# Branch B's product of a hybrid encoder step: out of the eight heads, into eight units of seven block products behind the merge gates

## The reference

```python
xr, gr, xm, zm, pi, pf, ga, gb = split(u @ w_in)       # 1024,1024,2048,2048,8,8,1024,1024
y_a = rglru(conv4(xr)) * gelu(gr)                       # 1024 wide
h_m = mlstm(q, k from silu(conv4(xm)), v from xm, pi, pf)   # 8 heads x 256
y_b = sigmoid(zm) * h_m                                 # 2048 wide
mix = sigmoid(ga) * (y_a @ w_branch_a) + sigmoid(gb) * (y_b @ w_branch_b)
x = x + mix @ w_out
x = x + relu(RMSNorm(x) @ w_mlp_up)**2 @ w_mlp_down     # then a final RMSNorm
```

## Time and profile before

| | us |
|---|---|
| median of 3 runs | 2144.64 (2144.36 to 2147.55) |
| the profiled execution, first to last instruction | 2142.7 |
| TensorE busy (share) | 2128.2 (99%) |
| VectorE busy | 1441.4 (67%) |
| POOL busy | 1093.8 (51%) |
| ScalarE busy | 715.3 (33%) |
| one head, from chunk stage to chunk stage | 100.94 |
| of it, the chain's stretch of 468 matmuls | 78.18 |

### The profile page before, as it was taken

The page is one execution under the profiler, slowest core; times in us unless marked ns, Lnnn a source line. Parts: engine busy times, 40 slices in busy tenths (PEclk is TensorE's granted clock), DMA queues, the critical chain, the costliest instruction groups (busy, mean ns, idle before and its releaser), DMA issues.

```text
span 2142.7 us, 37489 instructions
## 1 busy us (share of the span) xinstructions
PE 2128.2 (99%) x14272; PEld 2106.8 (98%) x14272; DVE 1441.4 (67%) x1522; ACT 715.3 (33%) x952; POOL 1093.8 (51%) x765
## 2 busy tenths in 40 slices
PE   9999999999999999999999999999999999999998
PEld 8999999999999999999999999999999999999988
DVE  7676776147767676867676756577876646458886
ACT  5443434213232322323232311234444434424342
POOL 3556564342434343433334244448787767778740
PEclk9999999999999999999999999999999999999999
DMA  3212112431212121111212123464445446526522
GB/s 134 71 55 69 61 55 98 148 102 56 68 45 67 45 78 58 54 58 50 62 50 62 45 96 97 149 227 174 173 166 182 152 167 250 198 100 244 184 70 84
DMA packets 95953, 230.50 MB, mean 108 GB/s; under 512 B 10464, under 2 KB 16736, under 8 KB 91392
## 3 DMA queue, kind: packets, MB, share of 16 engines
q1 hardware_dynamic: 58960, 109.03, 16.3%
q10 hardware_dynamic: 36912, 120.34, 15.3%
HBM read 168.52 MB, written 60.82 MB: 107 GB/s over the span
## 4 chain that ended last, share of the span: by engine, by line
PE 94%; DVE 3%; DMA 1%; POOL 1%; issue 1%; ACT 1%; DVEq 0%; SPq 0%; POOLq 0%; ACTq 0%
PE ps L916 56%; PE ps L1199 24%; PE ps L1296 4%; PE ps L1108 2%; PE ps L1142 1%; PE ps L1123 1%; PE ps L1145 1%; DMA last_x<-hid 1%; PE ps L1150 1%; PE ps L1094 1%; DVE form_lo L2050 0%; DVE vt L2047 0%; PE ps L1095 0%; DVE acc L2050 0%; POOL wsum L802 0%
## 5 line engine op out<-in xcount | busy, mean ns | idle before, releaser
L774 POOL TENSOR_TENSOR w_hi<-w_raw,ones 128x512 fp32r<-128x512 f32 x216 | 261.0, 1208 | 807.3 <-PE ps L916 761.4
L777 POOL TENSOR_TENSOR w_lo<-w_raw,w_hi 128x512 fp32r<-128x512 f32 x216 | 336.7, 1559 | 16.9
L916 PE MATMUL ps<-u_hi,w_hi 128*128 128x364 f32 x1521 | 337.8, 330 | 1.5 <-issue 0.6
L916 PE MATMUL ps<-u_hi,w_lo 128*128 128x364 f32 x1521 | 335.7, 329 | 0.0
L916 PE MATMUL ps<-u_lo,w_hi 128*128 128x364 f32 x1521 | 335.2, 328 | 0.0
L916 PEld LDWEIGHTS ps<-u_hi,w_hi 128*128 128x128 f32 x1521 | 263.8, 188 | 3.0 <-issue 1.2
L916 PEld LDWEIGHTS ps<-u_lo,w_hi 128*128 128x128 f32 x1521 | 264.5, 188 | 0.0
L916 PEld LDWEIGHTS ps<-u_hi,w_lo 128*128 128x128 f32 x1521 | 264.4, 188 | 0.0
L1199 PE MATMUL ps<-form_hi,hi 128*128 128x272 f32 x784 | 162.1, 288 | 0.4 <-POOL lo L799 0.4
L1199 PE MATMUL ps<-form_hi,lo 128*128 128x272 f32 x784 | 162.3, 288 | 0.0
L1199 PE MATMUL ps<-form_hi,w_hi 128*128 128x272 f32 x776 | 161.4, 289 | 0.8 <-DVE small L2050 0.4
(11 more groups left out here) (354 smaller groups left out, 4509.7 us busy)
## 6 DMA issues: line engine op xcount, KB each, us to landing
w_raw<-in_w SPq DMA_DIRECT2D x280, 256.0 KB, 2.6
form_lo<-hid_forms ACTq DMA_DIRECT2D x21, 1088.0 KB, 7.8
rstd<-in_w SPq DMA_DIRECT2D x50, 256.0 KB, 2.7
hid_forms<-acc ACTq DMA_DIRECT2D x12, 816.0 KB, 6.0
bc<-out_rows ACTq DMA_DIRECT2D x8, 1092.0 KB, 6.1
hid_forms<-stage ACTq DMA_DIRECT2D x6, 1088.0 KB, 4.4
hid_forms<-acc ACTq DMA_DIRECT2D x12, 544.0 KB, 7.0
hid_forms<-acc ACTq DMA_DIRECT2D x6, 1088.0 KB, 4.3
```

What stands on the lines that cost most here:

```text
L774: nc.gpsimd.tensor_tensor(w_hi[:, c, :], w_raw[:, c, :], one, ALU.mult).then_inc(s_whi, 1)
L777: nc.gpsimd.tensor_tensor(w_lo[:, c, :], w_raw[:, c, :], w_hi[:, c, :].bitcast(F32), ALU.subtract).then_inc(s_wlo, 1)
L916: mm = nc.tensor.matmul(slots[slot][:, t, :], w, r(k)[:, t * TW:(t + 1) * TW], start=(k == 0 and n == 0), stop=(k == last_k and n == 2))
```

## The change

- y no longer goes through branch B in the head. y = z * h is made in two rows of `acc` (`z_rows`) by one VectorE operation. ScalarE stores three of its quarters in DRAM (B11, B21, B22 of this head: two DMAs), POOL makes the four sums T1 to T4 by differences (`y_sum`), and ScalarE stores them. A form in DRAM is 128 x 8 heads x 546 columns.
- The z products of a head are made a head earlier, behind its xm products (`z_out`), those of head 0 ahead of the loop where the filler stood. The drain waits `m_c` and `m_oe` both stand ahead of the first product behind the chunks; before, `m_oe` stood between the first and the second. A head's loads fall from 14 chunks to 10.
- After the last head come seven gb products in a row (the eighth stays early); VectorE drains each into a row of `acc`, ScalarE takes the sigmoid and stores it (`gate_store`). The last two are interleaved by chunk.
- Then eight units of seven products (`b_multiply`, 4 K blocks x 3 terms x 2 matmuls of 274 and 272 columns), units 0 to 3 over heads 0 to 3, units 4 to 7 over heads 4 to 7, which add onto `acc`. All seven forms are loaded whole and split by ScalarE and VectorE (`b_form_hi`, `b_form_lo`), for units 4 to 7 beside units 3 and 4. Weights are loaded as raw blocks of 128 columns (`b_raw`, two DMAs each).
- The merge: rows times gate plus `mixa` (`mix_row`, 16 rows loaded through three buffers and four late ones), beside units 5 to 7, its low parts in unit 7 and behind it. w_out follows and waits for all but the last quarter of unit 7.
- Counts of semaphores that the MLP shares rise by constants.

The core of the diff:

```diff
@@ PE, a head
             pe.wait_ge(m_c, NCH * h + NCH)
-            c1 = c0 + 2
-            product(0, full(c1), *U)
             pe.wait_ge(m_oe, NCH * h + NCH)
-            product(1, full(c1 + 2), *U)
...
-            for m in range(KB):
...
-                product(m % 2, [(first, ws, off, False), (None, ws, off + P, m % 2 == 1)], *Y,
-                        before=lambda k: pe.wait_ge(m_ylo, 2 * h + k + 1), done=s_bb)
+            if not final:
+                pair_of(c0 + 2, a0 + 2, b0 + 2)
+                pair_of(c0 + 6, a0 + 3, b0 + 3)
@@ PE, the units
+        b_multiply(0, B11, 0)
+        pe.wait_ge(s_drA, A_WO)
+        for t in range(B_UNITS):
+            group, final = t // 4, t == B_UNITS - 1
+            if t:
+                pe.wait_ge(s_q, QUARTERS * t - 2)
+            b_multiply(b_index(t, P5), T1, group)
...
+            b_multiply(b_index(t, P6), T2, group)
...
+            b_multiply(b_index(t, P2), B21, group)
...
+            b_multiply(b_index(t, P7), T3, group)
+            pe.wait_ge(s_q, QUARTERS * t + 2)
+            if not final:
+                b_multiply(b_p1(t + 1), B11, (t + 1) // 4)
+            b_multiply(b_index(t, P3), B22, group)
+            pe.wait_ge(s_q, QUARTERS * t + 3)
+            b_multiply(b_index(t, P4), T4, group)
+        pe.wait_ge(s_q, QUARTERS * B_UNITS - 1)
@@ SP, behind the gb chunks
+        sp.wait_ge(s_chunk, W_GB + 14)
+        b_load(B22)
+        b_load(T4)
+        sp.wait_ge(g_st, 16 * KB)
+        b_row_load(0)
...
+        b_row_load(1)
+        b_row_load(2)
+        for t in range(1, B_UNITS + 1):
+            if t < B_UNITS:
+                if t > 1:
+                    sp.wait_ge(v_lo, b_index(t - 2, P4) + 1)
+                b_raw(b_raw22[t % 2][:], t, 3, r_raw22[t % 2])
+                sp.wait_ge(w_add, 4 * t - 1)
+                b_raw(raw11, t, 0, r_raw11)
...
+            if t > 5:
+                n = t - 6
+                for k in range(4 * n + 3, min(4 * n + 7, 12)):
+                    sp.wait_ge(f_row, k - 2)
+                    b_row_load(k)
@@ ACT, in unit t
+            b_weight_hi(b_index(t, P7), b_raw21[:])
+            b_step(t, 0)
+            if not final:
+                act.wait_ge(r_raw11, 32 * t + 64)
+                b_weight_hi(b_p1(t + 1), raw11)
+            b_step(t, 1)
@@ DVE, in unit t
+        def b_step(t, step):
+            f = {(0, 1): B22, (0, 2): T4, (3, 1): B11, (3, 3): T1, (3, 4): T2, (3, 5): B21,
+                 (4, 1): T3, (4, 2): B22, (4, 3): T4}.get((t, step))
+            if f is not None:
+                b_form_lo(int(t > 0), f)
+            if t >= 5 and step == 1:
+                mix_row(2 * (t - 5))
+                mix_row(2 * (t - 5) + 1)
...
+                b_quarter(t, P2, s1, s1, 2)
+                b_added(t, s1, n0, B_FIRST, 3, 1)
+                b_step(t, 2)
+                b_quarter(t, P7, s1, b_snap4, 2)
+                b_quarter(t, P7, s2, s2, 1)
+                b_added(t, s1, n1, B_SECOND, 4, 2)
+                b_step(t, 3)
+                if t == B_UNITS - 1:
+                    for n in range(4):
+                        mix_lo(n)
+                b_quarter(t, P3, b_snap4, b_snap4, 2)
+                b_added(t, b_snap4, n0, B_SECOND, 6, 3)
+                b_step(t, 4)
+                if t == B_UNITS - 1:
+                    mix_lo(4)
+                    mix_lo(5)
+                    mix_row(6)
+                b_quarter(t, P4, s2, s2, 5)
+                b_added(t, s2, n1, B_FIRST, 7, 4)
+                b_step(t, 5)
+        mix_row(7)
+        mix_lo(6)
+        mix_lo(7)
```

More of the change, by code:

```diff
@@ L232, in build @@
         last_x = sb_in(st, "last_x", [P, KB, 2, MC], F32R)
+    with ExitStack() as st:
+        b_low = [[sb_in(st, f"bform{f}_{part}", [P, 4, HB], F32R) for part in ("hi", "lo")] for f in range(4)]
+    with ExitStack() as st:
+        b_end_rows = sb_in(st, "b_end_rows", [P, 4, COLS])
     sb("u_space", [P, 2 * KB * COLS])
@@ L899, in _, with weight_block @@
     def _(pe):
-        def weight_block(slot, k, last_k, chunk, ws, off, last, rhs_hi, rhs_lo, before=None, done=None, parts=None,
-                         third_free=None):
+        def weight_block(slot, k, last_k, chunk, ws, off, last, rhs_hi, rhs_lo, before=None, done=None, parts=None):
             if chunk is not None:
@@ L2302, in _ @@
             ao(i, 1)
-        dve.wait_ge(w_st, 48)
-        for first, end in ((0, MASK), (MASK + 1, EE)):
-            V.memset(acc[:, first:end, :], 0.0).then_inc(s_zero, 1)
         def row_columns():
@@ new lines, in _, with b_quarter @@
+        dve.wait_ge(g_gb, 16)
+        tt(acc[:, EARLY_ROW, :], acc[:, EARLY_ROW, :], rstd[:], ALU.mult, g_u)
+        gb_out(0)
+        gb_out(1)
+        gb_out(2)
+        b_form_lo(0, B11)
+        gb_out(3)
+        b_form_lo(0, T1)
+        gb_out(4)
+        b_form_lo(0, T2)
+        gb_out(5)
+        gb_out(6)
+        b_form_lo(0, B21)
+        b_form_lo(0, T3)
+        def b_quarter(t, product, out, part, count):
+            q = b_index(t, product)
+            dve.wait_ge(s_mm, q + 1)
+            dve.wait_ge(s_q, QUARTERS * t + count)
+            tt(out, b_pairs[b_slot(q)], part, ALU.add, s_q)
@@ new lines, in b_added, with mix_row @@
+        def b_added(t, part, n, half, count, done):
+            dve.wait_ge(s_q, QUARTERS * t + count)
+            tt(acc[:, n, half], acc[:, n, half], part, ALU.add, b_acc)
+            dve.wait_ge(b_acc, 4 * (t - 4) + done)
+        def mix_row(n):
+            for k in (2 * n, 2 * n + 1):
+                buf, done, count = b_row_buf(k)
+                dve.wait_ge(done, count)
+                if k:
+                    dve.wait_ge(f_row, k)
+                tt(acc[:, n, :], acc[:, n, :], buf, (ALU.mult, ALU.add)[k % 2], f_row)
```

866 lines of the change are left out of this document (552 added, 314 removed).

## The result

The changed kernel takes 2160.47 us (median of 4 runs, 2158.55 to 2163.68) against 2144.88 for the kernel before (4 runs, 2144.36 to 2147.55): a ratio of 1.0072, 95% interval 1.0058 to 1.0087, 15.6 us slower. The forecast was 2144.0 in a range of 2134 to 2156, so it is wrong, and on the side of rivals 2 and 3. The profiled execution is the slowest of the four: 2163.68 us, span 2161.5.

What follows compares the result with a forecast made beforehand. TensorE was taken to bound the kernel. Matmuls -23.0, convolution cover -0.9, heads +4.8, first unit +3.5, units 3 and 4 +4.0, last unit +11.0 sum to -0.6: forecast 2144.0 us, range 2134 to 2156.

Steps and rivals of the forecast that it cites:

- Rival 2: Unit 7 and merge: VectorE becomes the bound, end costs 19.5 us in place of 11; +12.2, total 2156.8; chance 0.20.
- rival 3: Heads: the cover of 2 to 5 us is short by 1, seven times; +7 us, total 2151; chance 0.06.
- The matmuls: Branch B: 1152 matmuls (192.4 us) go, 1344 at 0.1260 us (169.4 us) come; net -23.0 us.
- The heads: Heads: first convolution's cover -0.9 us, moved drain wait +4.8 us, the shorter head still covered.
- POOL's four new differences of y: Heads: they fall between splits that wait for TensorE and cost nothing.
- The moved wait: Head's end: both drain waits ahead of the next product, 0.6 us x 8 heads = +4.8 us (4 to 5.6).
- Is the shorter head covered?: Heads: VectorE's work ends at 43 to 46 us, TensorE's products at 48.1; some 2 to 5 us left.
- A longer period means rival 3: Sign in the heads: they should repeat every 77.5 us; a longer period would show rival 3.
- Unit 0: First unit: unit 1's raw weights come late behind the gate stores and row loads; +3.5 us (0.5 to 6).
- Unit 4: Units 3 and 4: VectorE's splits make operands late; +4.0 us (0 to 7).
- The end: Last unit and w_out: w_out starts 6.4 late, 2.9 more within, POOL's splits 1.7; +11.0 us (9 to 19).
- rival 4: w_out may start at the lower clock after TensorE idles; up to +6 us, total 2150; chance 0.04.

Runs made afterwards that it cites:

- the width run: Changed kernel with every unit matmul but the first term's writing 272 columns instead of 274 and 272: 2163.68 us (2 runs), ratio 1.0087.
- VectorE's order alone: Changed kernel with merge rows 4 and 5 formed behind unit 6 and unit 7's third quarter sum ahead of low parts: 2157.71 us, 1.0059.
- the version with everything: Changed kernel plus three head edits (z drain, POOL differences, ScalarE wait), SyncE's order at unit 0, VectorE's and SyncE's at the end: 2143.51 us, 0.9994.

## Why the prediction was wrong

**The matmuls: right in kind, 2.5 us short.** The units' matmuls cost 0.1279 in place of 0.1260; my price came from columns alone, and the width run shows that columns explain 0.0008 of the 0.0023 above the MLP's 0.1256.

**The heads: the step that failed.** The sum put POOL at nothing: "POOL's four new differences of y fall between splits that wait for TensorE: nothing." Two of them stand in a row ahead of one split, 2.2 to 2.4 us each beside VectorE, and make its low part late: 0.38 us of idleness a head, 0.64 from start to start, 4.5 us over seven heads. Spreading them took that stretch away. The moved wait was right in kind (+4.8) and cost 5.8, as a stretch costs more than it idles. Together that is the 5.5 by which the heads missed.
A second step was wrong too, though in the changed kernel it cost nothing by itself. "Is the shorter head covered?" counted convolution and splitting and found 2 to 5 us left. It left out VectorE's two copies of z out of PSUM, 1.28 and 1.30, made behind `xc_lo`, on the first of which the next k product waits; and it took operations beside POOL at the old pace. What was left was 0.4 us, and only because TensorE was late itself. So the cure of POOL's order gained 0.31 us a head in place of 0.64, and the cure of the moved wait nothing. "A longer period means rival 3" was therefore wrong as a sign: the period was longer, 78.3 for 77.5, without any product waiting for VectorE. Rival 3's mechanism shows only in the versions with POOL's sums spread or ScalarE's wait moved.

**Unit 0: right place, right queue, half the size.** 5.6 for my 3.5, and 1.8 at the low clock that I left out. The mis-sized term is the store of the last gate row: 6 to 8 after the last gb matmul in my count, 10 by the trace. Two operands load beside it (DMA engines 0.73 busy from 1160 to 1171); that they are what slowed it wasn't tested apart. My upper end was 6.

**Unit 4: right.** 4.0 forecast, 3.7 seen, in three stretches behind the low parts of the operands, as written. The 4.0 was a choice between two ends taken from the rows and not a sum, so that it came so near is in part luck. The Trainium skill's exclusive lock (SBUF — State Buffer, "SBUF: two separate sides"), by which the prediction had worked out 7, is seen in the single durations (2.3 for 1.2) but overstates their sum here.

**The end: right in kind, 2.6 us short.** w_out started 7.4 late for my 6.4, waited 2.7 within for my 2.9, and 3.3 went to the low clock, rival 4's mechanism, in a smaller size than its 6. I took VectorE's row operations at uncontended prices: four low parts took 6.83 us where 5.2 stood. The Trainium skill (TensorE: Matmul & The Clock Gate, "What's actually happening") says that the clock drops to half on idleness; here it did so behind stretches of 5.6, 7.4 and 2.7 us, and I should have put it into the sum and not only among the rivals.

**The MLP: left out**, some 3 us, cause open.

The misses are heads 5.5, unit 0 3.9, end 2.6, matmuls 2.5, MLP about 3: five terms, all of one sign. Most queues were counted with the durations of a kernel in which they had room. Rival 2's total, 2156.8, was nearest, but its reason, an end of 19.5 us, was not the one.

## What to carry to other kernels

When a change shortens a loop that TensorE bounds, write out the other engines' chain through one turn, from the last thing it waits for to the release of the slot that the next turn needs, with every copy out of PSUM in it; the saving is lost if that chain is longer, and two chains of nearly equal length hide each other, so that neither cure pays much alone. A queue that waits for a store before it issues loads should have nothing urgent behind that wait. Where VectorE is busy without a gap, reordering its queue moves the stretches of TensorE and not the end.

## What was not expected of the hardware

The granted clock can fall behind short stretches: with TensorE idle for 2.75 us ahead of w_out (VectorE's order alone) the slice 1345 to 1350 is at 0.68. But a stretch of 2.9 us at the same place, in the version with everything, left it at 1.00 from 1332 to 1340, so the length of the stretch alone doesn't decide. Stretches of 0.4 to 1.7 us in unit 4 left it at 1.00. A store of 0.56 MB took 3.2 us in the median before and 5.9 here (`gb_gates`). Copies out of PSUM stayed at 0.71 to 0.73 us beside POOL, while a 128x1092 difference within SBUF took 1.3 alone and 2.2 to 2.4 beside it.
